# A merged value operand, one channel summed on GpSimd, and row sums inverted by chunk in an attention kernel

## The chip, the cores and the metric

One core of a Trainium2 chip. The metric is the device time of one execution in microseconds (us), lower is better. The engines are TensorE (PE in the rows; PEld is its weight load), VectorE (DVE), ScalarE (ACT), GpSimd (POOL) and SyncE (SP), which here issues the DMAs of the attention.

## The reference, cut to what matters

One step of a hybrid encoder: a combined input projection, a short gated convolution, a forgetting attention, and an output projection with a norm. The change touches the attention over the 2,048 prompt rows, for 8 heads of 64 channels:

```
logits = einsum('bqhd,bkhd->bhqk', q, k) * scale
logits = logits + cq[..., None] - ck[:, :, None, :]
logits = where(k_pos <= q_pos, logits, -inf)
att = einsum('bhqk,bkhd->bqhd', softmax(logits), v)
y_b = att * silu(z_b)
```

## The kernel before, in words

The program has two stages. The first makes the projections and writes q, k and v, each split into a high and a low part, to DRAM. The second runs the prompt attention, then the attention of 32 sample rows over a cache (`sample_attention`), the merge and the output norm. All matrix products take split operands: high x high, high x low and low x high.

`prompt_attention` runs over heads h = 0 to 7. A head has NS = 40 steps (q, kb): four chunks q of QW = 512 queries, and for each the key blocks kb = 0 to 4q + 3 of 128 keys. So the chunks take 4, 8, 12 and 16 steps, and `ends` = (3, 11, 23, 39) are their last steps. The last four key blocks of a chunk lie on the diagonal and are narrower (512, 384, 256 and 128 columns). In a step

- TensorE (`tensor`) makes the logits of step st + 3 (`scores`, two passes), units of the row maxima of the *next* head (`unit`, 40 a head, spread over steps 0 to 29, in two banks `m_bank` by turns), and then the values of step st (`values`, three passes into `o_bank[q % 2]`);
- ScalarE (`probs`) takes the exponential of a step twice: rounded into `p_hi`, and full into the logits' own bank;
- VectorE makes the low part (`low`, into `p_lo`), reduces the units, and at the end of a chunk copies the output out of PSUM (`take`).

p_hi, p_lo and the logits' banks are rings of RING = 4. The value operand `v_hi` holds 64 channels of high values and columns of ones, so that row 64 of the output is the sum of the probabilities; `v_lo` holds 64 channels of low values and zeros.

The row sums must be inverted and spread over 64 partitions. That goes through DRAM on SyncE's queue: `sum_store` (a row of 512 sums to DRAM), `sums_load` (back as 128 x 16), `invert` on VectorE (step INVERT = 9 of the next head), `rcp_store`, `rcp_load` (broadcast). Then GpSimd and ScalarE finish the head in steps 20 to 37 of the next one: `scale`, `gate`, `upper` (high part) and `lower` (low part); `y_store` writes both parts.

SyncE works through its list strictly in the order written in `sync`: a DMA behind a wait, or behind a DMA whose issue is held, waits too. `load_main(h + 1)` loads keys, queries and values of the next head, `load_max(h + 2)` what the row maxima of the head after need. Lines of the program before, with the profile's numbers: L1531 and L1533 are the loads of `load_main`, L1525 those of `load_max`, L1502 the sum store, L1507 and L1515 the loads of sums and reciprocals, L1605 to L1607 the value passes, L1588 and L1589 the logits, L1621 a unit, L1667 and L1668 the exponentials, L1698 the low part, L1706 the reduction of a unit, L1651 `upper`, L1767 to L1776 GpSimd's finishing, L1901 the cached keys for the sample part.

Of the kernel before, what the change touches and what calls it, by code (L numbers as in the profile page):

```python
# [23 lines left out]
H = 8  # L24
# [177 lines left out]
def front(nc, held, s, g_out, lead, x_prompt, x_sample, ln_in, w_tiles, w_f, b_f, conv_w, cache_logf, state_conv, ident, causal,  # L202
          k_prompt, v_prompt, logf_prompt, conv_prompt, k_sample, v_sample, logf_sample, conv_sample):
    with ExitStack() as ctx:
# [148 lines left out]
        def _(sp):  # L353
# [139 lines left out]
            for i in range(NSETS + 2):  # L493
# [90 lines left out]
                if i == 2 * PER + 19:  # L584
                    load_lead_v(0, s["vh"])
# [747 lines left out]
        def _(pool):  # L1333
# [16 lines left out]
            pool.memset(v0[0][:, :, HD:P].bitcast(F32), 1.0).then_inc(lead_ones, 1)  # L1350
            for idx in (0, 2, 5):
                pool.wait_ge(w_lo[idx], NSETS - 1)
            pool.memset(v0[1][:, :, HD:P].bitcast(F32), 0.0).then_inc(lead_ones, 1)
# [58 lines left out]
def prompt_attention(nc, held, s, g_out, lead, causal):  # L1412
    st_ = Stage()
    with ExitStack() as ctx:
# [21 lines left out]
        v_hi, v_lo = (main[:, :, 2 + x].rearrange("p a (b c) -> p a b c", c=P) for x in range(2))  # L1436
# [16 lines left out]
        o_read = sem("o_read")  # L1453
        sum_out, sums_in, rcp_done, rcp_out, rcp_in = (
            sem("sum_out"), sem("sums_in"), sem("rcp_done"), sem("rcp_out"), sem("rcp_in"))
# [15 lines left out]
        INVERT = 9  # L1471
        FINISH = {20 + 4 * q + x + x // 2: (q, x) for x in range(3) for q in range(NQ)}
        FINISH_LOW = {st + 5: q for st, (q, x) in FINISH.items() if x == 0}
        TURN = 32

# [24 lines left out]
        def sum_store(sp, h, q):  # L1500
            sp.wait_ge(o_read, NQ * h + q + 3)
            sp.dma_start(s["sums"][h:h + 1, q * QW:(q + 1) * QW], y[HD:HD + 1, h % 2, q * QW:(q + 1) * QW])\  # L1502
              .then_inc(sum_out, 16)

        def sums_load(sp, h):
            sp.wait_ge(sum_out, 64 * h + 64)
            sp.dma_start(sums[:, :], s["sums"][h:h + 1, :].rearrange("a (p b) -> (a p) b", p=P)).then_inc(sums_in, 16)  # L1507

        def rcp_store(sp, h):
            sp.wait_ge(rcp_done, h + 1)  # L1510
            sp.dma_start(s["rcps"][h:h + 1, :].rearrange("a (p b) -> (a p) b", p=P), rcp[:, :]).then_inc(rcp_out, 16)

        def rcp_load(sp, h):
            sp.wait_ge(rcp_out, 16 * h + 16)
            sp.dma_start(rcp_all[:, :], s["rcps"][h:h + 1, :].broadcast_to([HD, SEQ])).then_inc(rcp_in, 16)  # L1515
# [4 lines left out]
        def sync(sp, sam):  # L1520
# [6 lines left out]
            def load_main(h):  # L1527
# [4 lines left out]
                for to, of in ((v_hi, s["vh"]), (v_lo, s["vl"])):  # L1532
                    sp.dma_start(to[:, b, :, 0:HD].bitcast(F32), of[0:SEQ, rows].rearrange("(b p) c -> p b c", p=P))\  # L1533
                      .then_inc(main_in[b], 16)

            for h in range(H):
                if h == 0:
                    sp.dma_start(mask[:, :], causal).then_inc(const_in, 16)
                if h:
                    sum_store(sp, h - 1, 3)  # L1540
                    sums_load(sp, h - 1)
                    rcp_store(sp, h - 1)
                    rcp_load(sp, h - 1)
                sp.dma_start(zb[:, h % 2], s["zb"][h * HD:(h + 1) * HD, 0:SEQ]).then_inc(zb_in[h % 2], 16)
                if h + 1 < H:
                    if h:
                        sp.wait_ge(pv_done, NS * h + RING)
                    load_main(h + 1)
# [6 lines left out]
                if h == H - 1:  # L1555
                    sam.key_loads(sp)
                sum_store(sp, h, 0)
                sum_store(sp, h, 1)
                if h:
                    y_store(sp, h - 1, 0)  # L1560
                sum_store(sp, h, 2)
                if h:
                    y_store(sp, h - 1, 1)
                if h + 1 < H:
                    max_rows(sp, h + 1)
                if h:
                    y_store(sp, h - 1, 2)
                    y_store(sp, h - 1, 3)

        def tensor(pe):  # L1570
            def scores(h, b, st):
# [4 lines left out]
                if st == 0:  # L1576
# [5 lines left out]
                    if h:  # L1582
                        pe.wait_ge(main_in[b], used(h, 2, 96))
                        pe.wait_ge(m_in[h % 3], used(h, 3, 32))
# [9 lines left out]
            def values(h, b, st):  # L1594
# [3 lines left out]
                if h == 0 and st == 0:  # L1598
                    pe.wait_ge(lead.v_in, 32)
                if kb == 0:  # L1600
# [27 lines left out]
            def head(h, b, more=True, ahead=True):  # L1628
                for st in range(NS):
# [9 lines left out]
                    values(h, b, st)  # L1639

# [3 lines left out]
            for h in range(H):  # L1644
                head(h, h % 2, h < H - 1, h < H - 1)

# [8 lines left out]
        def scalar(act):  # L1655
# [5 lines left out]
            def probs(h, st):  # L1661
# [4 lines left out]
                act.wait_ge(pv_done, NS * h + st + 1)  # L1666
                act.activation(p_hi[:, r, cols], s_bank[r][:, cols], ACT.Exp, scale=SCALE)  # L1667
                act.activation(s_bank[r][:, cols], s_bank[r][:, cols], ACT.Exp, scale=SCALE).then_inc(p_done, 1)  # L1668

# [6 lines left out]
            for h in range(H):  # L1676
                for st in range(NS):
# [3 lines left out]
                    if st in FINISH and FINISH[st][1] == 2 and h:  # L1681
                        upper(act, h - 1, 1 - h % 2, FINISH[st][0])

        def invert(dve, h):
            dve.wait_ge(sums_in, 16 * h + 16)
            if h:
                dve.wait_ge(rcp_out, 16 * h)
            dve.reciprocal(rcp[:, :], sums[:, :]).then_inc(rcp_done, 1)
# [3 lines left out]
        def vector(dve, sam):  # L1692
# [32 lines left out]
            def take(h, b, q):  # L1725
                dve.wait_ge(pv_done, NS * h + ends[q] + 1 + RING)
                if h > 1:
                    dve.wait_ge(yl_done, NQ * (h - 1))
                dve.tensor_copy(y[:, b, q * QW:(q + 1) * QW], o_bank[q % 2][0:HD + 1, :]).then_inc(o_read, 1)

            def head(h, b, more=True):
                for st in range(NS):
# [9 lines left out]
                    if st - 2 in ends[:-1]:  # L1742
                        take(h, b, ends.index(st - 2))
                    if b and st == 1:
                        take(h - 1, 1 - b, NQ - 1)
                    if st == INVERT and h:
                        invert(dve, h - 1)
                if b:
                    take(h, b, NQ - 1)

            dve.memset(wide_mask[:, 0:QW - P], 0.0).then_inc(mask_made, 1)
# [4 lines left out]
            for h in range(H):  # L1756
# [3 lines left out]
                head(h, h % 2, h < H - 1)  # L1760

        def scale(pool, h, b, q):
            if q == 0:
                pool.wait_ge(rcp_in, 16 * h + 16)
                pool.wait_ge(zb_in[b], 16 * (h // 2 + 1))
# [15 lines left out]
        def gpsimd(pool, sam):  # L1781
# [3 lines left out]
            pool.memset(v_hi[:, 1, :, HD:P].bitcast(F32), 1.0).then_inc(ones_set, 1)  # L1785
            pool.memset(v_lo[:, 1, :, HD:P].bitcast(F32), 0.0).then_inc(ones_set, 1)
# [3 lines left out]
            for h in range(1, H):  # L1790
                for st in range(NS):
                    if st in FINISH_LOW:
                        lower(pool, h - 1, 1 - h % 2, FINISH_LOW[st])
                    if st in FINISH and FINISH[st][1] < 2:
                        (scale, gate)[FINISH[st][1]](pool, h - 1, 1 - h % 2, FINISH[st][0])
# [5 lines left out]
def sample_attention(nc, held, s, att, cache_k, cache_v, blocks):  # L1801
    me = Stage()
    with ExitStack() as ctx:
# [206 lines left out]
        def vector(dve, mrg):  # L2010
# [15 lines left out]
            for c in range(NP):  # L2026
# [5 lines left out]
                if c == 0:  # L2032
                    att.invert(dve, H - 1)
# [517 lines left out]
def tail_loads(sp, s, att, sam, mrg, out):  # L2551
# [3 lines left out]
    att.sums_load(sp, h)  # L2555
    sam.load_v(sp, 1)
    att.rcp_store(sp, h)
    sam.load_v(sp, 2)
    att.rcp_load(sp, h)
# [97 lines left out]
```

## Time and profile before

| | |
|---|---|
| median of 3 runs | 1916.48 us (1916.2 to 1919.73) |
| profiled execution | 1916.35 us |
| its span on the core | 1914.3 us |
| TensorE busy | 1864.5 us, 97% |
| VectorE busy | 1294.4 us, 68% |
| ScalarE busy | 854.5 us, 45% |
| GpSimd busy | 186.0 us, 10% |
| prompt attention | about 1074 to 1484 us of the span |

Shares are averages over stages with different limits, so the rows of the prediction are taken from the attention alone. TensorE's matmuls are pipelined: a matmul's own time is longer than the distance of two starts, and the distance is what one costs.

### The profile page before, as it was taken

To read this page: it belongs to the slowest core of one execution; us is meant where nothing else is said; L and a number is where in the kernel's file an instruction comes from. 1 tells how busy PE (TensorE), PEld (TensorE's weight loads), DVE (VectorE), ACT (ScalarE), POOL (GpSimd) and SP (SyncE) were. 2 spreads that over 40 slices of the span, in tenths; PEclk is the share of its full clock that TensorE was granted. 3 is DMA by queue.
4 is the path that set the end of the run, shared out by engine and by line. 5 is a ranking of instruction groups with operands and counts; after the bars stand their busy time and mean duration, and the time that the engine had idled before them with its cause. 6 is when DMAs were issued, how large, how long until landed. Compare 5 with 4: busy or idle time off the path is not lost. (4 is left out here: it accounts for less than half of the span.)

```text
span 1914.3 us, 28697 instructions
## 1 busy us (share of the span) xinstructions
PE 1864.5 (97%) x10592; PEld 1725.4 (90%) x10592; DVE 1294.4 (68%) x2256; ACT 854.5 (45%) x1592; POOL 186.0 (10%) x153
## 2 busy tenths in 40 slices
PE   5999999999999999999999999999999999999998
PEld 4999999999999999999999787887788799998885
DVE  7888787954445455544556588889996644457887
ACT  4554555634343444424323577777779700111100
POOL 1000000000000000000000203333323400000111
PEclk8999999999999999999999999999999999999999
DMA  5698898878888886979897906666655697765441
GB/s 200 233 316 303 313 315 297 304 244 307 276 312 295 294 283 230 297 231 325 259 305 237 232 11 133 134 133 134 128 106 147 205 377 245 246 181 162 143 146 72
DMA packets 272782, 435.99 MB, mean 228 GB/s; under 512 B 63252, under 2 KB 139188, under 8 KB 268508
## 3 DMA queue, kind: packets, MB, share of 16 engines
q1 hardware_dynamic: 266884, 425.64, 70.8%
q10 hardware_dynamic: 5760, 8.52, 1.2%
q8 instruction: 85, 1.39, 0.3%
q14 instruction: 53, 0.43, 0.1%
HBM read 285.18 MB, written 148.78 MB: 227 GB/s over the span
## 5 line engine op out<-in xcount | busy, mean ns | idle before, releaser
L781 ACT ACTIVATE fr_wq<-fr_raw 128x512 fp32r<-128x512 f32 x288 | 178.9, 629 | 209.8 <-PE fr_d L625 137.6
L1698 DVE TENSOR_TENSOR at_p_lo<-at_s,at_p_hi 128x512 fp32r<-128x512 f32 (+1 forms) x320 | 192.1, 604 | 42.8 <-ACT at_s L1668 41.2
L1667 ACT ACTIVATE at_p_hi<-at_s 128x512 fp32r<-128x512 f32 (+1 forms) x320 | 170.3, 532 | 83.5 <-PE at_s L1589 49.2
L1045 DVE TENSOR_TENSOR fr_wq<-fr_raw,fr_wq 128x512 fp32r<-128x512 f32 x288 | 192.5, 684 | 9.6 <-ACT fr_wq L781 6.3
L623 PE MATMUL fr_b<-fr_xh,fr_wq 128*128 128x348 f32 x576 | 188.1, 327 | 6.9 <-DVE fr_u L1152 3.9
L623 PE MATMUL fr_c<-fr_xh,fr_wq 128*128 128x348 f32 x576 | 187.5, 325 | 3.8 <-DVE fr_wq L1045 2.8
L623 PE MATMUL fr_a<-fr_xh,fr_wq 128*128 128x348 f32 x576 | 187.2, 325 | 2.2 <-ACT fr_p L854 2.2
L624 PE MATMUL fr_a<-fr_xl,fr_wq 128*128 128x348 f32 x576 | 186.7, 324 | 0.0
L624 PE MATMUL fr_c<-fr_xl,fr_wq 128*128 128x348 f32 x576 | 186.1, 323 | 0.0
L625 PE MATMUL fr_a<-fr_xh,fr_wq 128*128 128x348 f32 x576 | 186.1, 323 | 0.0
L625 PE MATMUL fr_b<-fr_xh,fr_wq 128*128 128x348 f32 x576 | 186.0, 323 | 0.0
L625 PE MATMUL fr_c<-fr_xh,fr_wq 128*128 128x348 f32 x576 | 185.8, 323 | 0.0
L624 PE MATMUL fr_b<-fr_xl,fr_wq 128*128 128x348 f32 x576 | 185.7, 322 | 0.0
L1668 ACT ACTIVATE at_s<-at_s 128x512 f32<-128x512 f32 (+1 forms) x320 | 169.4, 529 | 0.0
L1204 DVE TENSOR_TENSOR fr_res<-fr_c,fr_u 128x348 f32<-128x348 f32 x72 | 37.5, 521 | 182.5 <-PE fr_c L625 182.3
L1605 PE MATMUL at_o<-at_p_hi,at_main 128*128 128x512 f32 (+1 forms) x320 | 123.4, 386 | 0.5
L915 ACT ACTIVATE fr_res<-fr_a 128x348 f32<-128x348 f32 x72 | 33.2, 462 | 193.7 <-PE fr_a L625 186.4
L1706 DVE TENSOR_REDUCE at_piece_max<-at_m 128x1 f32<-128x512 f32 x168 | 114.4, 684 | 6.2 <-PE at_m L1621 5.9
L1588 PE MATMUL at_s<-at_main 128*128 128x512 f32 (+1 forms) x320 | 117.5, 367 | 0.2 <-issue 0.2
L1589 PE MATMUL at_s<-at_qm,at_km 68*128 68x512 f32 (+1 forms) x320 | 117.7, 368 | 0.0
L1606 PE MATMUL at_o<-at_p_lo,at_main 128*128 128x512 f32 (+1 forms) x320 | 117.4, 367 | 0.0
L1607 PE MATMUL at_o<-at_p_hi,at_main 128*128 128x512 f32 (+1 forms) x320 | 117.2, 366 | 0.0
(360 smaller groups left out, 4652.8 us busy)
## 6 DMA issues: line engine op xcount, KB each, us to landing
fr_wq<-w_mixed SPq DMA_DIRECT2D x192, 512.0 KB, 5.4
fr_raw<-w_tiles SPq DMA_DIRECT2D x96, 512.0 KB, 5.3
w_mixed<-fr_wq SPq DMA_DIRECT2D x96, 512.0 KB, 4.6
mg_gates<-merge_gates SPq DMA_DIRECT2D x40, 416.0 KB, 4.8
fr_raw<-w_tiles SPq DMA_DIRECT2D x48, 256.0 KB, 5.7
merge_gates<-fr_res SPq DMA_DIRECT2D x32, 348.0 KB, 6.4
mixed<-mg_mixed ACTq DMA_DIRECT2D x40, 208.0 KB, 4.1
ln_h<-h_rows SPq DMA_DIRECT2D x16, 512.0 KB, 3.2
```

The lines of the kernel that those rows point to most:

```text
L623: pe.matmul(to, wh[:, idx, k, :], xh[:, idx, k, :], start=first, stop=False, skip_group_check=skip)
L624: pe.matmul(to, wh[:, idx, k, :], xl[:, idx, k, :], start=False, stop=False, skip_group_check=skip)
L625: last = pe.matmul(to, wl[:, idx, k, :], xh[:, idx, k, :], start=False, stop=end, skip_group_check=skip)
L781: act.activation(wh[:, idx], operand(i, idx), ACT.Copy).then_inc(w_hi[idx], 1)
L1045: dve.tensor_tensor(wl[:, idx], operand(i, idx), wh[:, idx].bitcast(F32), ALU.subtract).then_inc(w_lo[idx], 1)
L1588: pe.matmul(bank[:, cols], ks[:, b, keys], qs[:, b, asked], start=True, stop=False)
L1589: last = pe.matmul(bank[:, cols], km[h % 3][:, keys], qm[h % 3][:, asked], start=False, stop=not diagonal)
L1605: pe.matmul(o, v_hi[:, b, kb, :], p_hi[:, r, cols], start=(kb == 0), stop=False)
L1606: pe.matmul(o, v_hi[:, b, kb, :], p_lo[:, r, cols], start=False, stop=False)
L1667: act.activation(p_hi[:, r, cols], s_bank[r][:, cols], ACT.Exp, scale=SCALE)
L1668: act.activation(s_bank[r][:, cols], s_bank[r][:, cols], ACT.Exp, scale=SCALE).then_inc(p_done, 1)
L1698: dve.tensor_tensor(p_lo[:, r, cols], s_bank[r][:, cols], p_hi[:, r, cols].bitcast(F32), ALU.subtract)\
```

## The change

Part one joins the operands. `v_both` holds 64 channels of high values, one column of ones, and channels 1 to 63 of the low values. One pass with p_hi and one with p_lo give high values, row sums and 63 low channels. `v_first` holds the low channel 0 and zeros, and is multiplied by p_hi in a third pass as before, except in the "pooled" steps: those below the diagonal with odd kb (kb = 1, 3 for q = 1, up to 1, 3, ..., 11 for q = 3). There GpSimd multiplies p_hi by the channel (`first_channel`) and adds it up in `acc`; one matmul a chunk q = 1, 2, 3 (`close`) sums `acc` over the partitions into the output bank.

Part two: the low rows now lie on partitions 64 to 127 of the output. ScalarE copies them to `part` (`copy_part`), and VectorE's `take` adds them to the high rows. `part` is one buffer; row 64 of it is what `sum_store` sends.

Part three: sums are loaded, inverted, stored and spread by chunk, with tables of steps for each job, and SyncE's list has a new order.

```diff
+                for to, of in ((v_both[:, b, :, 0:HD], s["vh"][0:SEQ, rows]),
+                               (v_both[:, b, :, HD + 1:P], s["vl"][0:SEQ, h * HD + 1:(h + 1) * HD]),
+                               (v_first[:, b, :, 0:1], s["vl"][0:SEQ, h * HD:h * HD + 1])):
...
             for h in range(H):
...
-                if h:
-                    sum_store(sp, h - 1, 3)
-                    sums_load(sp, h - 1)
-                    rcp_store(sp, h - 1)
-                    rcp_load(sp, h - 1)
+                if h > 1:
+                    sp.wait_ge(y_gated, NQ * (h - 1))
                 sp.dma_start(zb[:, h % 2], s["zb"][h * HD:(h + 1) * HD, 0:SEQ]).then_inc(zb_in[h % 2], 16)
                 if h + 1 < H:
                     if h:
-                        sp.wait_ge(pv_done, NS * h + RING)
+                        sp.wait_ge(closed, 3 * h)
                     load_main(h + 1)
                 if h + 2 < H:
...
                     load_max(h + 2)
                 if h == 1:
                     sam.early_loads(sp)
                 if h == H - 1:
                     sam.key_loads(sp)
+                if h:
+                    sum_store(sp, h - 1, 3)
+                    y_store(sp, h - 1, 1)
+                    y_store(sp, h - 1, 2)
+                    sums_load(sp, h - 1, 3)
                 sum_store(sp, h, 0)
+                sums_load(sp, h, 0)
+                if h:
+                    rcp_store(sp, h - 1, 3)
+                    rcp_load(sp, h - 1, 3)
+                rcp_store(sp, h, 0)
                 sum_store(sp, h, 1)
...
-                pe.matmul(o, v_hi[:, b, kb, :], p_hi[:, r, cols], start=(kb == 0), stop=False)
-                pe.matmul(o, v_hi[:, b, kb, :], p_lo[:, r, cols], start=False, stop=False)
-                pe.matmul(o, v_lo[:, b, kb, :], p_hi[:, r, cols], start=False, stop=(kb == 4 * q + 3))\
-                  .then_inc(pv_done, 1)
+                pe.matmul(o, v_both[:, b, kb, :], p_hi[:, r, cols], start=(kb == 0), stop=False)
+                last = pe.matmul(o, v_both[:, b, kb, :], p_lo[:, r, cols], start=False, stop=False)
+                if not pooled(st):
+                    last = pe.matmul(o, v_first[:, b, kb, :], p_hi[:, r, cols], start=False, stop=(q == 0 and kb == 3))
+                last.then_inc(pv_done, 1)
+
+            def close(h, q):
...
+                pe.wait_ge(acc_done, added_through(h, q))
+                pe.matmul(o_bank[q % 2][:, :], first_row[:, :], acc[:, :], start=False, stop=True).then_inc(closed, 1)
...
                     values(h, b, st)
+                    if h and st == 0:
+                        close(h - 1, NQ - 1)
+                    if st - 1 in ends[1:-1]:
+                        close(h, ends.index(st - 1))
...
+                if before[0] >= 0 and pooled(before[1]):
+                    act.wait_ge(acc_scaled, pooled_through(*before))
...
+            def copy_part(h, q):
+                n = NQ * h + q
...
+                act.wait_ge(o_read, n + 2)
+                act.wait_ge(sum_out, 16 * n)
+                act.activation(part[HD:2 * HD, :], o_bank[q % 2][HD:2 * HD, :], ACT.Copy).then_inc(part_done, 1)
...
             def take(h, b, q):
-                dve.wait_ge(pv_done, NS * h + ends[q] + 1 + RING)
+                dve.wait_ge(part_done, NQ * h + q + 1)
...
-                dve.tensor_copy(y[:, b, q * QW:(q + 1) * QW], o_bank[q % 2][0:HD + 1, :]).then_inc(o_read, 1)
+                o = o_bank[q % 2]
+                dve.scalar_tensor_tensor(out=y[0:HD, b, q * QW:(q + 1) * QW], in0=part[HD:2 * HD, :], scalar=lanes[HD:2 * HD, :],
+                                         in1=o[0:HD, :], op0=ALU.mult, op1=ALU.add).then_inc(o_read, 1)
```

The tables, as (head back, chunk) by step: `copy_part` stands at steps 8, 16, 28 and, for chunk 3, step 4 of the next head; `take` at 7, 15, 27 and 3; `invert` at 15, 23, 35 and 12 of the next head; scale, gate, upper and lower of chunk 0 at 24, 25, 28 and 29, the others in steps 0 to 23 of the next head.

In SyncE's list, this is the turn of one head in the middle of the attention, before. `at_main` is what `load_main` fills, `at_km` and `at_qm` belong to `load_max`:

```order
L1502 DMA sums<-at_y 1x512
L1507 DMA at_sums<-sums 128x16
L1511 DMA rcps<-at_rcp 128x16
L1515 DMA at_rcp_all<-rcps 64x2048
L1544 DMA at_zb<-silu_zb 64x2048
L1531 DMA at_main<-k_hi 64x2048
```

And now, from the first load of the head to the first sum stores:

```order
L1574 DMA at_zb<-silu_zb 64x2048
L1562 DMA at_main<-k_hi 64x2048
L1562 DMA at_main<-q_lo 64x2048
L1562 DMA at_main<-k_lo 64x2048
L1562 DMA at_main<-q_hi 64x2048
L1566 DMA at_main<-v_hi 128x16x64
L1566 DMA at_main<-v_lo 128x16x63
L1566 DMA at_main<-v_lo 128x16x1
L1556 DMA at_km_51<-k_hi 64x2048
L1556 DMA at_qm_53<-q_hi 64x2048
L1556 DMA at_km_51<-forget_rows 2x2048
L1528 DMA sums<-at_part 1x512
```

The store of the previous head's last sums, first of the head before, now stands behind its loads, and there is one load more (`v_lo 128x16x1`).

On ScalarE, before, around steps 7, 8 and 9 of a head there are only exponentials (a 512 pair, the 512 pair of step 8, the 384 pair of step 9):

```order
L1668 ACTIVATE at_s<-at_s 128x512
L1667 ACTIVATE at_p_hi<-at_s 128x512
L1668 ACTIVATE at_s<-at_s 128x512
L1667 ACTIVATE at_p_hi<-at_s 128x384
L1668 ACTIVATE at_s<-at_s 128x384
```

And now at the same place:

```order
L1727 ACTIVATE at_s<-at_s 128x512
L1726 ACTIVATE at_p_hi<-at_s 128x512
L1727 ACTIVATE at_s<-at_s 128x512
L1737 ACTIVATE at_part<-at_o 64x512
L1726 ACTIVATE at_p_hi<-at_s 128x384
L1727 ACTIVATE at_s<-at_s 128x384
```

The copy of chunk 0 has come between the exponentials of steps 8 and 9, with the waits of `copy_part`.

## Rows read from the trace of the kernel before

**Rows 1.** Head 3 in stretches: busy PE, PEld, DVE, ACT, POOL; granted clock, DMA.
```profile
1235.80:1248.00 12.20, 12.15 (x64) 9.87 (x63) 11.48 (x32) 7.98 (x19) 0.00 (x0) 1.00 0.01 2
1248.00:1261.60 13.60, 13.60 (x67) 11.01 (x67) 13.34 (x30) 10.68 (x21) 3.83 (x3) 1.00 0.76 161
1261.60:1276.80 15.20, 15.20 (x71) 12.15 (x71) 14.59 (x30) 12.36 (x25) 8.66 (x7) 1.00 1.10 210
1276.80:1287.70 10.90, 10.81 (x61) 8.50 (x59) 6.90 (x16) 8.71 (x22) 2.71 (x3) 1.00 0.33 91
```

**Rows 2.** Timeline of TensorE in head 2: start, duration (us).
```profile
1217.59 0.40 PE L1605 MATMUL at_o<-at_p_hi,at_main 128*128 128x512 f32 x1
...
1218.06 0.39 PE L1607 MATMUL at_o<-at_p_hi,at_main 128*128 128x512 f32 x1
```

**Rows 3.** Timeline of SyncE's queue in head 3: start and time of issue.
```profile
1251.73 0.59 SPq L1531 DMA_DIRECT2D at_main<-k_hi  x1
...
1254.93 12.66 SPq L1533 DMA_DIRECT2D at_main<-v_lo  x1
...
1271.12 0.54 SPq L1502 DMA_DIRECT2D sums<-at_y  x2
```

**Rows 4.** DMA issues of 1199 to 1235 us: size, time to landing (us).
```profile
at_rcp_all<-rcps SPq DMA_DIRECT2D x1, 512.0 KB, 4.7
...
at_main<-k_hi SPq DMA_DIRECT2D x1, 512.0 KB, 8.6
...
at_main<-v_hi SPq DMA_DIRECT2D x1, 512.0 KB, 16.0
at_main<-v_lo SPq DMA_DIRECT2D x1, 512.0 KB, 18.6
```

**Rows 5.** Groups of ScalarE and VectorE by shape: busy us, mean ns.
```profile
L1706 DVE TENSOR_REDUCE at_piece_max<-at_m 128x1 f32<-128x512 f32 x168 | 114.4, 684 | 6.2 <-PE at_m L1621 5.9
...
L1698 DVE TENSOR_TENSOR at_p_lo<-at_s,at_p_hi 128x384 fp32r<-128x384 f32 x32 | 17.7, 553 | 1.4 <-ACT at_s L1668 0.3
...
L1651 ACT ACTIVATE at_y_hi<-at_y 64x512 fp32r<-64x512 f32 x32 | 19.6, 618 | 0.0
...
L1668 ACT ACTIVATE at_s<-at_s 128x384 f32<-128x384 f32 x32 | 15.5, 486 | 0.0
```

**Rows 6.** GpSimd's `lower`: shortest, median and longest duration (ns).
```profile
L1776 POOL TENSOR_TENSOR at_y_lo<-at_y,at_y_hi x32: 1278/1284/2335, 1159.6 to 1521.6; 64x512 fp32r<-64x512 f32 x32
```

**Rows 7.** Waits of SyncE in the attention: total us, times, longest.
```profile
SPq L1507 <- DMA sums<-at_y: 6.3, 7, 0.9
```

**Rows 8.** Timeline of TensorE in head 3: first value pass, step 9's first unit.
```profile
1235.85 0.45 PE L1605 MATMUL at_o<-at_p_hi,at_main 128*128 128x512 f32 x1
...
1247.82 0.40 PE L1621 MATMUL at_m<-at_km,at_qm 66*128 66x512 f32 x1
```

**Rows 9.** Timeline of TensorE where the attention stage begins, with its idle before.
```profile
1073.95 0.22 PE L1641 MATMUL at_m<-at_eye_b,at_mask_b 128*128 128x128 bf16 x1 [3.42 <-PEq L65]
```

**Rows 10.** Stretches of 2 us in head 0, columns as in rows 1.
```profile
1078.00:1080.00 2.00, 2.00 (x5) 1.70 (x6) 0.65 (x4) 0.36 (x2) 1.37 (x2) 0.50 1.15 326
1080.00:1082.00 2.00, 2.00 (x7) 1.81 (x6) 0.64 (x3) 1.09 (x2) 1.85 (x2) 0.52 1.09 225
1082.00:1084.00 2.00, 2.00 (x13) 1.74 (x12) 1.35 (x5) 1.39 (x3) 0.42 (x1) 1.00 1.00 205
```

**Rows 11.** Timeline of SyncE's queue in head 1, from the early loads on.
```profile
1166.88 1.28 SPq L1889 DMA_DIRECT2D sa_q_hi<-q_hi  x2
...
1174.76 0.35 SPq L1502 DMA_DIRECT2D sums<-at_y  x1
```

**Rows 12.** Timeline of SyncE's queue in head 7.
```profile
1454.90 4.71 SPq L1901 DMA_DIRECT2D sa_k_rows<-cache_k  x4
...
1464.12 0.56 SPq L1502 DMA_DIRECT2D sums<-at_y  x2
```

**Rows 13.** Line L1901, the cached keys: issue to landing.
```profile
DMA to landing us min/median/max: 9.3/12.5/17.4
```

More of the change, by code:

```diff
@@ L1435, in prompt_attention @@
         ks, qs = main[:, :, 0], main[:, :, 1]
-        v_hi, v_lo = (main[:, :, 2 + x].rearrange("p a (b c) -> p a b c", c=P) for x in range(2))
+        v_both, v_first = (main[:, :, 2 + x].rearrange("p a (b c) -> p a b c", c=P) for x in range(2))
+        first_row = sb("first_row", [P, P], 29184, F32R)
+        acc = sb("acc", [P, QW], 29312, F32R)
+        lanes = sb("lanes", [P, 1], 29824)
+        part = sb("part", [P, QW], 34880)
+        term = sb("term", [P, QW], 29832)
         s_bank = [pb(f"s{i}") for i in range(RING)]
@@ L1469, in step_units, with pooled, pooled_through, added_through @@
             return range(min(NU, st * 4 // 3), min(NU, (st + 1) * 4 // 3))
-        INVERT = 9
-        FINISH = {20 + 4 * q + x + x // 2: (q, x) for x in range(3) for q in range(NQ)}
-        FINISH_LOW = {st + 5: q for st, (q, x) in FINISH.items() if x == 0}
-        TURN = 32
+        INVERT = {15: (0, 0), 23: (0, 1), 35: (0, 2), 12: (1, 3)}
+        SCALE_AT = {24: (0, 0), 0: (1, 1), 2: (1, 2), 18: (1, 3)}
+        GATE_AT = {25: (0, 0), 1: (1, 1), 3: (1, 2), 19: (1, 3)}
+        UPPER_AT = {28: (0, 0), 4: (1, 1), 6: (1, 2), 22: (1, 3)}
+        LOWER_AT = {29: (0, 0), 5: (1, 1), 7: (1, 2), 23: (1, 3)}
+        PART_AT = {(e + 5) % NS: (0 if e + 5 < NS else 1, q) for q, e in enumerate(ends)}
+        TAKE_AT = {(e + 4) % NS: (0 if e + 4 < NS else 1, q) for q, e in enumerate(ends)}
+        TURN = 32
+        def pooled(st):
+            q, kb = steps[st]
+            return kb < 4 * q and kb % 2 == 1
+        def pooled_through(h, st):
+            return sum(map(pooled, range(NS))) * h + sum(map(pooled, range(st + 1)))
+        def added_through(h, q):
+            return pooled_through(h, ends[q]) - 3 * h - q
+        def at_step(plan, h, st):
+            back, q = plan.get(st, (0, None))
+            h -= back
+            return (h, q) if q is not None and h >= 0 else None
         def used(h, slots, per):
@@ L1741, in head @@
                             whole_max(h + 1)
[L1742 to L1749, printed above, removed]
+                    job = at_step(TAKE_AT, h, st)
+                    if job:
+                        take(job[0], job[0] % 2, job[1])
+                    if at_step(INVERT, h, st):
+                        invert(dve, *at_step(INVERT, h, st))
+            dve.memset(lanes[:, :], 1.0).then_inc(lanes_set, 1)
+            dve.wait_ge(lanes_set, 1)
+            dve.memset(lanes[HD:HD + 1, :], 0.0).then_inc(lanes_set, 1)
+            dve.wait_ge(lanes_set, 2)
             dve.memset(wide_mask[:, 0:QW - P], 0.0).then_inc(mask_made, 1)
@@ L1784, in gpsimd @@
             pool.wait_ge(ones_set, 2)
[L1785 to L1786 removed]
+            pool.memset(v_both[:, 1, :, HD:HD + 1].bitcast(F32), 1.0).then_inc(ones_set, 1)
+            pool.memset(v_first[:, 1, :, 1:P].bitcast(F32), 0.0).then_inc(ones_set, 1)
+            pool.memset(first_row[:, 1:P].bitcast(F32), 0.0).then_inc(first_row_set, 1)
+            pool.memset(first_row[:, 0:1].bitcast(F32), 1.0).then_inc(first_row_set, 1)
             for q in g_out:
@@ L2032, in vector @@
                 if c == 0:
[L2033 removed]
+                    att.invert(dve, H - 1, NQ - 1)
                 if c:
```

139 lines of the change are left out of this document (92 added, 47 removed).

## Prediction

> **What bounds the kernel now.** I read the busy time of one head by stretches first. Attention runs eight heads of 40 steps; head 3 (counted from 0) takes the 51.9 us from 1235.8, cut at its steps 9, 19 and 30 [rows 1]. TensorE is busy 51.76 of 51.90 us at full granted clock, so it sets the pace. VectorE is right behind in steps 9 to 29: 13.34 of 13.60 and 14.59 of 15.20 us, which leaves 0.87 us. ScalarE has 2.2 us left in the last ten steps; GpSimd is nearly idle. Then the timeline of TensorE: two passes of 512 columns lie 1217.59 to 1218.06 apart, so one costs 0.235 us [rows 2].
>
> Then SyncE's queue, which looks harmless now [rows 3]. The loads for head 4 begin at 1251.73, the issue of v_lo holds the queue for 12.66 us, and the store of row sums behind them is issued at 1271.12, after 19.4 us. The landing times say why: k_hi, q_lo, k_lo and q_hi move first and v_hi lands 16.0 us after its own issue [rows 4]; the queue takes v_lo's 2,048 small pieces only as those before them drain. Nobody waits for that store today: `take` has copied the sums to `y`, and the inversion comes a head later.
>
> **The change part by part.**
>
> *Passes.* A step below the diagonal with odd kb loses its third value pass: 2 + 4 + 6 = 12 of 40. Three closings per head come back. Net 9 x 0.235 = 2.1 us a head, 16.9 us in all, if nothing else binds. In steps 9 to 29 seven passes go and two closings come (1.2 us), where VectorE has 0.87 us and gets three more small inversions; I keep 0.6 there, 0.24 in steps 0 to 8, 0.55 of 0.7 at the end beside ScalarE. That is 1.4 a head: **11 us gained** (ends 5 and 16.9).
>
> *ScalarE and VectorE.* `copy_part` moves 64x512 out of PSUM, near the 64x512 ACTIVATE of 0.62 us [rows 5]; four a head, in ScalarE's idle time except where it waits (below). `take` stays one 512-wide VectorE instruction. Nothing for either.
>
> *GpSimd.* A pooled step costs a multiply and an add of 128x512. Nearest row: 64x512 two-input, median 1.28 us [rows 6]. Steps 24 to 35 ask for 6 multiplies, 5 adds and 3 finishing operations: 14 x 1.3 = 18.2 us, against about 13.2 us of TensorE. ScalarE comes back to a slot of the ring of four after four steps (4.8 us); less the multiply itself, GpSimd may be about 3.5 us late. At 1.3 us a multiply it would be 5.0 late: 1.5 us a head, 12 in all. At half that price a multiply (one input) costs 0.65 and nothing stalls. I take nothing, with 0 and 12 as ends.
> The Trainium skill (GPSIMD Engine Reference, section Elementwise — side-by-side cycle accounting) gives a two-input operation about 2.6 cycles per element, which would be 1.1 us (the row shows 1.28), and a one-input loop at best 769 ns for 512 elements. By that estimate the stretch asks 15.0 us, nothing stalls and the sum stays as below; by 1.3 us for both it is 12 us more.
>
> *The order of SyncE's queue; this decides.* Now the loads of head h+1 stand first in head h, and the store of the last row sums of head h-1 behind them. `part` is one buffer: `copy_part` of (h, 0), which stands on ScalarE after step 8, waits until all 4h earlier stores have landed. That store cannot be issued before the loads, and the loads wait for the last closing of head h-1, which TensorE does in step 0 of head h. From the first value pass of head h, in us:
> - three passes, the closing and its end: SyncE is released at 1.2;
> - the loads: 19.4 as now [rows 3], less 3.9, since rcp_all and zb are no longer in front (k_hi lands 8.6 after its issue, a 512 KB transfer with an empty queue 4.7 [rows 4]), plus the new load of 2,048 pieces of 4 bytes. No row has that. v_lo's 2,048 pieces of 256 bytes land 2.6 after v_hi's and were issued 0.63 later: 3.2. Ends: 0 and 6; I take 3.0, near the row with as many pieces. So 18.5: the store is issued at 19.7;
> - it lands 1.1 later (0.2 of issue, 0.9 of SyncE's wait [rows 7]): 20.8;
> - ScalarE's copy 0.6: 21.4. Behind it stand the two exponentials of step 9 (384 wide, 0.49 each, overlapping: 0.9): 22.3. VectorE, held in `take`, then makes p_lo (0.55): 22.85, and reads unit 10 (0.6): 23.4 [rows 5].
>
> TensorE cannot pass: the values of step 9 need that p, and its first unit of step 9 needs unit 10's bank. Now it comes to that unit at 1247.82, 12.0 after 1235.85 [rows 8]; two passes fewer make it 11.5. So TensorE stands **11.9 us in each head**. After an idle of 3.42 us at the change of stages [rows 9] the granted clock was half (1.2 GHz): 5 and 7 matmuls in two windows of 2 us at 0.50 and 0.52, then 13 in one at 1.00 [rows 10]. That is some 2 us lost; after a stall VectorE is late as well and hides a little of it. I add 1.7 us a stall (ends 0 and 2): 13.6.
>
> *Which heads.* Heads 2 to 6: 5 x 13.6 = 68.0. Head 1 has the early loads of the sample part ahead of the store too, 1166.88 to 1174.76 = 7.9 [rows 11]: 21.5. Head 7 loads cached keys instead, 9.2 from the first key load to the store [rows 12], so the store goes out 10.4 sooner; with no units TensorE is at step 9 about 2 sooner: 3.4. There the inversion of (6, 3) on VectorE in step 12 waits for sums that lie behind 4 MB of keys, the last of which lands 17.4 after its issue [rows 13]: about 3 more. 6.5 together (0 to 12).
>
> *Edges.* One more small load ahead of head 0 and a copy ahead of the last `take`: about 1 us each (0 to 3 together). Head 0 has no earlier store to wait for.
>
> **Sum.** 68.0 + 21.5 + 6.5 + 2 - 11 = +87. The profiled execution took 1916.35 us (span 1914.3 and 2.05 around it), as good as the median of 1916.48. So **2003 us**. Its ends: with 0 for the 4-byte load, no loss of clock, the full gain and nothing in head 7 or at the edges, the idle is 8.9 and the sum 6 x 8.9 + 7.9 - 16.9 = +44 (1961). With 6 for it, half the relief, 2 of clock, 5 gained and 12 in head 7, it is 6 x 18.8 + 7.9 + 12 + 3 - 5 = +131 (2047).
>
> **Rivals.**
> - *It does what it says.* The queue takes the loads at once when nothing is in front, the store is out in time, and the gain less the edges is left: 1916 - 9 = 1907. It decides where the loads are issued within 18.5 - 11.9 = 6.6 us of the closing. For it: seven loads at 0.6 us would be 4.2. Against: four transfers of 512 KB, landing some 2.5 us apart, still stand before v_hi. 9%.
> - *The queue blocks, but half as long*, because it is empty at the start: issued after 12 instead of 18.5, TensorE stands 5.4 us: 6 x 5.4 + 7.9 + 3 + 2 - 11 = +34, 1950. For: the block is data, and 1 MB less is ahead. Against: 1 MB was worth 3.9 us and is already off. 9%.
> - *GpSimd becomes the bound.* The longest two-input operation took 2.34 us [rows 6]. If all did, steps 24 to 35 would ask 14 x 2.3 = 32 against 13, 15 us a head past what the ring forgives: 120 on top, 2123. Against: the median is 1.28 while VectorE was nine tenths busy. 5%. The Trainium skill (GPSIMD Engine Reference, Key points) says that GpSimd shares its SBUF interfaces with VectorE and contends with VectorE instructions that have two SBUF inputs; those of the steps have one input in PSUM, and by that rule they do not slow it.
>
> **How the numbers follow.** The forecast with its ends has 75%, the three rivals 9, 9 and 5, and 2% is left for what I do not see. Likeliest 2003, alone 1961 to 2047; the range goes down to 1940 to take in the half block and up to 2045. About 0.2% (4 us) is what a measurement of this kernel can tell from no change. Slower by more: 0.89; within: 0.02; faster: 0.09.
>
> **What would show it.** Right: in heads 1 to 6 an idle of 9 to 17 us on TensorE before the first unit of step 9, ScalarE's `at_part` copy of (h, 0) waiting for the DMA of `sums`, SyncE's issue of the v loads still held 8 us or more, heads of about 64 us, and a granted clock near 0.5 for some us after each. Also 96 value passes fewer, 24 closings, the multiply on GpSimd under 1.3 us. Wrong: the store of (h-1, 3) issued within 7 us of the closing, or POOL named as what ScalarE waits for.

## The result and the profile after

| | before | after |
|---|---|---|
| median of 4 runs each, same chip | 1916.34 us (1915.47 to 1919.73) | 2081.43 us (2079.32 to 2082.36) |
| ratio, 95% interval | | 1.086 (1.0845 to 1.0875) |
| span of the profiled execution | 1914.3 us | 2080.5 us |
| mean granted clock of TensorE | 0.989 | 0.953 |
| GpSimd busy | 186.0 us | 426.9 us |

The change costs 165 us. The forecast was 2003, from 1940 to 2045: the sign and the place were right, the size about half.

The first value pass of each head, in the timeline of TensorE, gives the length of the heads. Head 7 and the last column are divided at the first value pass of its last step. The lower lines are kernels of the experiments.

| us | head 0 | 1 | 2 | 3 | 4 | 5 | 6 | 7 | rest |
|---|---|---|---|---|---|---|---|---|---|
| before | 53.3 | 52.4 | 51.9 | 52.0 | 51.9 | 51.9 | 51.8 | 40.5 | 430.3 |
| after | 63.2 | 79.7 | 74.8 | 75.5 | 75.2 | 74.3 | 67.8 | 57.4 | 433.5 |
| e5, only SyncE's list mended | 55.7 | 57.4 | 56.8 | 56.8 | 56.8 | 57.1 | 58.3 | 49.3 | 431.9 |
| e6, copy of chunk 3 earlier | 55.9 | 57.1 | 56.5 | 56.5 | 56.4 | 56.7 | 56.5 | 49.5 | 435.2 |
| e7, and no channel on GpSimd | 55.2 | 53.9 | 55.3 | 54.8 | 54.7 | 54.4 | 54.3 | 41.5 | 436.4 |
| e11, list mended again | 54.5 | 53.4 | 55.3 | 53.3 | 53.4 | 53.4 | 53.2 | 42.6 | 432.1 |
| e12, before with the new order | 54.3 | 68.3 | 65.3 | 64.9 | 64.9 | 66.7 | 59.2 | 49.2 | 433.9 |

All but some 4 us of the loss lies in the attention. Its third value pass of 512 columns runs 128 times in place of 224, and 24 closings have come, as foretold. Head 3 in stretches, cut by what happens there (columns as in [rows 1]):

```profile
1297.00:1308.80 11.80, 10.69 (x55) 8.59 (x56) 9.67 (x26) 7.81 (x17) 10.45 (x9) 1.00 0.85 182
1308.80:1325.40 16.60, 1.43 (x7) 0.85 (x6) 2.13 (x4) 2.88 (x9) 0.37 (x1) 0.64 0.90 161
1325.40:1334.40 9.00, 9.00 (x27) 7.56 (x28) 5.83 (x14) 3.78 (x8) 0.23 (x1) 0.53 0.02 3
```

For nearly 15 us hardly any engine works, only the DMA engines do (0.90 of their time), and then TensorE runs some 9 us at a granted clock near half. SyncE's queue in the same head (start, time of issue), to hold against [rows 3]:

```profile
1298.16 0.45 SPq L1562 DMA_DIRECT2D at_main<-k_hi  x1
...
1301.21 11.68 SPq L1566 DMA_DIRECT2D at_main<-v_lo  x2
1312.93 2.25 SPq L1556 DMA_DIRECT2D at_km<-k_hi  x1
...
1316.35 0.25 SPq L1528 DMA_DIRECT2D sums<-at_part  x1
...
1322.41 0.35 SPq L1533 DMA_DIRECT2D at_sums<-sums  x1
```

The sum store of head 2's last chunk is issued 18.2 us after the first load. Four stores of finished parts follow it without a wait (1316.65 to 1319.05, not shown); the load of those sums, which waits for it to land, goes out at 1322.41: the store of 2 KB took 6.1 us. What it holds up, in the timelines of ScalarE, VectorE and TensorE (in brackets the idle before):

```profile
1322.49 0.59 ACT L1737 ACTIVATE at_part<-at_o 64x512 f32<-64x512 f32 x1 [16.72 <-DMA sums<-at_part]
...
1323.12 0.74 DVE L1803 SCALAR_TENSOR_TENSOR at_y<-at_part,at_lanes,at_o 64x512 f32<-64x512 f32 x1 [14.79 <-ACT at_part L1737]
1324.02 0.56 DVE L1771 TENSOR_TENSOR at_p_lo<-at_s,at_p_hi 128x384 fp32r<-128x384 f32 x1 [0.15 <-ACT at_s L1727]
1324.49 0.68 DVE L1779 TENSOR_REDUCE at_piece_max<-at_m 128x1 f32<-128x512 f32 x1
...
1325.23 0.79 PE L1672 MATMUL at_m<-at_km,at_qm 66*128 66x512 f32 x1 [15.17 <-DVE at_piece_max L1779]
```

This is the chain of the forecast, link by link: store, copy, addition, low part, unit, TensorE. The long idles of the heads that differ from head 3 (heads 0, 1, 6 and 7, the last with two):

```profile
1108.82 0.80 PE L1672 MATMUL at_m<-at_km,at_qm 66*128 66x512 f32 x1 [4.34 <-DVE at_piece_max L1779]
...
1174.88 0.79 PE L1672 MATMUL at_m<-at_km,at_qm 66*128 66x512 f32 x1 [17.81 <-DVE at_piece_max L1779]
...
1544.29 0.80 PE L1672 MATMUL at_m<-at_km,at_qm 66*128 66x512 f32 x1 [9.27 <-DVE at_piece_max L1779]
...
1607.17 0.69 PE L1649 MATMUL at_o<-at_p_hi,at_main 128*128 128x384 f32 x1 [5.54 <-DVE at_p_lo L1771]
...
1626.88 0.33 PE L1649 MATMUL at_o<-at_p_hi,at_main 128*128 128x128 f32 x1 [3.98 <-DVE at_p_lo L1771]
```

Head 0, which was to have no stall, has one at step 17: its own first store stands behind the loads, and the copy of chunk 1 waits for that. GpSimd's groups, to hold against [rows 6]:

```profile
L1886 POOL TENSOR_SCALAR at_term<-at_p_hi,at_main 128x512 f32<-128x512 f32 x72 | 112.6, 1564 | 11.5 <-ACT at_s L1727 6.1 <-POOL at_acc L1888 5.5
L1888 POOL TENSOR_TENSOR at_acc<-at_acc,at_term 128x512 fp32r<-128x512 f32 x72 | 92.7, 1287 | 6.0
L1881 POOL TENSOR_SCALAR at_acc<-at_p_hi,at_main 128x512 fp32r<-128x512 f32 x24 | 37.6, 1567 | 192.7 <-PE at_o L1659 173.0 <-ACT at_s L1727 19.7
```

The multiply costs 1.56 us, more than the two-input addition of 1.29. ScalarE's waits for GpSimd in the attention (total us, times, longest):

```profile
ACT at_y_hi L1707 <- POOL at_y L1849: 31.1, 14, 5.2
...
ACT at_p_hi L1726 <- POOL at_term L1886: 14.8, 10, 1.9
```

The first is `upper`, which waits for a part that GpSimd has gated, the second an exponential that waits for its slot of the ring.

### The profile page after: what moved, and what is told of

It is laid out like the page before. It is cut to its first block and busy times, and to the rows that moved or that the text cites. A ratio compares the mean times of both kernels' runs of the same rounds, so it can differ in the third digit from the quotient of the medians.

```text
span 2080.5 us, 29040 instructions
## 1 busy us (share of the span) xinstructions
PE 1896.1 (91%) x10520; PEld 1737.7 (84%) x10520; DVE 1313.8 (63%) x2282; ACT 868.2 (42%) x1624; POOL 426.9 (21%) x323
## 5 line engine op out<-in xcount | busy, mean ns | idle before, releaser
L1771 DVE TENSOR_TENSOR at_p_lo<-at_s,at_p_hi 128x512 fp32r<-128x512 f32 (+1 forms) x320 | 193.0, 605 | 68.3 <-ACT at_s L1727 66.2
L1672 PE MATMUL at_m<-at_km,at_qm 66*128 66x512 f32 (+2 forms) x280 | 112.7, 427 | 102.6 <-DVE at_piece_max L1779 102.6
L626 PE MATMUL fr_b<-fr_xh,fr_wq 128*128 128x348 f32 x576 | 186.0, 323 | 0.0
L1672 PEld LDWEIGHTS at_m<-at_km,at_qm 66*128 66x128 f32 x280 | 57.6, 208 | 128.9 <-DVE at_piece_max L1779 118.7
L1649 PE MATMUL at_o<-at_p_hi,at_main 128*128 128x512 f32 (+1 forms) x320 | 130.5, 408 | 29.0 <-DVE at_p_lo L1771 21.8
L1338 POOL TENSOR_TENSOR fr_small<-fr_small 128x1 f32<-128x1 f32 (+1 forms) x18 | 12.4, 688 | 622.3 <-DVE fr_small L1021 622.3
L1632 PE MATMUL at_s<-at_main 128*128 128x512 f32 (+1 forms) x320 | 124.1, 388 | 0.0
L1633 PE MATMUL at_s<-at_qm,at_km 68*128 68x512 f32 (+1 forms) x320 | 123.5, 386 | 0.0
```

Source lines behind the costliest of these rows:

```text
L626: last = pe.matmul(to, wl[:, idx, k, :], xh[:, idx, k, :], start=False, stop=end, skip_group_check=skip)
L1632: pe.matmul(bank[:, cols], ks[:, b, keys], qs[:, b, asked], start=True, stop=False)
L1649: pe.matmul(o, v_both[:, b, kb, :], p_hi[:, r, cols], start=(kb == 0), stop=False)
L1672: pe.matmul(bank[:, 0:width], qm[h % 3][0:HD + 2, i * P:(i + 1) * P], km[h % 3][0:HD + 2, c * QW:end], start=True, stop=True).then_inc(uni ...
L1771: dve.tensor_tensor(p_lo[:, r, cols], s_bank[r][:, cols], p_hi[:, r, cols].bitcast(F32), ALU.subtract)\
```

## The experiments

Theory A: the order of SyncE's list makes the loss, through the late store. B: the added work on GpSimd and VectorE makes it. C: the single buffer `part` makes it. D: the store lands late whatever stands ahead of it. Times are medians of 4 runs; the kernel before, run beside each of them on the same chip, stood at 1915.5 to 1916.7.

**e12, the order alone in the kernel before.**

```diff
-                if h:
-                    sum_store(sp, h - 1, 3)
-                    sums_load(sp, h - 1)
-                    rcp_store(sp, h - 1)
-                    rcp_load(sp, h - 1)
-                sp.dma_start(zb[:, h % 2], s["zb"][h * HD:(h + 1) * HD, 0:SEQ]).then_inc(zb_in[h % 2], 16)
...
                     load_main(h + 1)
...
                     load_max(h + 2)
...
                     sam.key_loads(sp)
+                if h:
+                    sum_store(sp, h - 1, 3)
+                    sums_load(sp, h - 1)
+                    rcp_store(sp, h - 1)
+                    rcp_load(sp, h - 1)
+                sp.dma_start(zb[:, h % 2], s["zb"][h * HD:(h + 1) * HD, 0:SEQ]).then_inc(zb_in[h % 2], 16)
```

> The kernel before, and of the whole change only the order in SyncE's list: the loads for the next heads stand ahead of the store, load and spreading of the last head's sums. Theory A (the order by itself makes the greater part of the loss): the sums come back some 25 us into each head, VectorE inverts them at step 9 (about 12 us in) and waits, TensorE stands 10 to 14 us in heads 1 to 6 and runs some us at half clock after it: 1990 to 2040 us. Rival (the order costs nothing without the copy that waits for the store): 1916, no change.

Measured: 2003.89 us, ratio 1.0453 (1.0432 to 1.0473). Nothing but the list is changed, and 88 us are lost. (`zb` comes last here; in the change it comes first.) SyncE's queue, VectorE and TensorE in head 3:

```profile
1281.98 0.25 SPq L1502 DMA_DIRECT2D sums<-at_y  x1
1287.91 0.35 SPq L1507 DMA_DIRECT2D at_sums<-sums  x1
...
1289.55 0.25 DVE L1688 RECIPROCAL at_rcp<-at_sums 128x16 f32<-128x16 f32 x1 [11.38 <-DMA at_sums<-sums]
...
1290.60 0.80 PE L1621 MATMUL at_m<-at_km,at_qm 66*128 66x512 f32 x1 [11.03 <-DVE at_piece_max L1706]
```

Without `part` and its copy it is the inversion of step 9 that waits. TensorE stands 14.0 us in head 1, 11.0 to 11.6 in heads 2 to 5 and 5.2 in head 6, which has no `load_max`. Theory A holds: which instruction waits differs between the kernels, the late sums do not.

**e2, four buffers, the list as changed.**

```diff
-        part = sb("part", [P, QW], 34880)
+        parts = [sb(f"part{i}", [P, QW], 34880 + i * QW) for i in range(NQ)]
...
-                act.wait_ge(sum_out, 16 * n)
+                act.wait_ge(sum_out, 16 * max(0, n - 3))
```

> The changed kernel with four buffers for the low rows, one for each chunk, so that ScalarE's copy waits only for the store four copies back. SyncE's list is as in the changed kernel. Theory A (the order of the queue): the copy no longer waits, but the sums of the last chunk still come back some 27 us after the head begins, and VectorE, which inverts them at step 12 (about 15 us in), takes the wait over: some 11 us of idle a head in place of 15, about 2050 us (2030 to 2070). Rival C (the one buffer is the cause): the stalls are gone and the time is about 1950 us.

Measured: 2024.59 us, ratio 1.0575 (1.0556 to 1.0595): 57 us better than the change and far from rival C, but 25 better than theory A's 2050 and below its range, since TensorE's idle is some 8 us and not 11. What wait is left went where A put it. VectorE and TensorE in head 3:

```profile
1305.12 0.18 DVE L1761 RECIPROCAL at_rcp<-at_sums 128x4 f32<-128x4 f32 x1 [8.11 <-DMA at_sums<-sums]
...
1306.32 0.80 PE L1672 MATMUL at_m<-at_km,at_qm 66*128 66x512 f32 x1 [7.65 <-DVE at_piece_max L1782]
```

**e4, only the loads for the maxima behind the store.**

```diff
-                if h + 2 < H:
...
-                    load_max(h + 2)
...
                     sum_store(sp, h - 1, 3)
+                    if h + 2 < H:
+                        load_max(h + 2)
```

> The changed kernel, only the loads for the row maxima (two of 512 KB and a small one) stand behind the store of the last sums instead of ahead of it (in head 0 behind the first store). Theory A, with the store landing late because 1 MB stands ahead of it in the same queue: in heads 1 to 5 the store is issued 3.4 us sooner and lands in 1 to 2 us instead of 6.1, so the idle at step 9 falls from 15 to about 7 us and the time to about 2040 us (2025 to 2050). Rival D (the store lands 6 us after its issue whatever stands just ahead): only the 3.4 us come back, 15 to 20 us in all, about 2062 us.

Measured: 2050.01 us, ratio 1.0705 (1.0688 to 1.0723), at the upper edge of A's range; D's 2062 lies outside the interval. SyncE, ScalarE and TensorE in head 3:

```profile
1296.55 1.86 SPq L1528 DMA_DIRECT2D sums<-at_part  x1
...
1300.16 0.59 ACT L1738 ACTIVATE at_part<-at_o 64x512 f32<-64x512 f32 x1 [9.88 <-DMA sums<-at_part]
...
1302.89 0.79 PE L1673 MATMUL at_m<-at_km,at_qm 66*128 66x512 f32 x1 [8.33 <-DVE at_piece_max L1780]
```

From the start of the store's issue to the copy it is now 3.6 us (1.9 of them held issue), not 6.1, and TensorE's idle is 8.3, not 15.2. So what stands ahead in the queue delays not only the issue but also the landing. Head 6, which has no such loads in the changed kernel either, stood 9.27 there. The stores of finished parts behind it do not make the delay: e12 has none there, and its store took 5.9.
The Trainium skill (DMA: Bandwidth & Descriptors, section Queues, rings and completion order) says that SyncE owns one row of rings and that each DMA engine takes that row's descriptors in order. By that rule the small store is taken up after the loads ahead of it; the 6.1 and 3.6 us agree.

**e1, the loads moved behind the stores.** The order of a head is now: last sums of the head before (store, load), `load_max`, sums of chunks 0 and 1, then the block `zb` and `load_main`, then the `y_store`s, sums of chunk 2, `max_rows`.

> Only SyncE's list is changed: the last sums of the head before are stored and loaded first, then come the two large loads for the row maxima, and the gate values and the keys, queries and values of the next head wait until the sums of chunk 1 have been stored and loaded (step 16). Every engine's work is that of the changed kernel. Theory A (the order of the queue makes the loss): ScalarE's copy never waits for a store, TensorE's idle of 15 us at step 9 goes and with it some 4 us of half clock behind it, so a head of 75 takes about 56 and the program 1940 to 1970 us. Rival B (the added work on GpSimd and VectorE makes the loss): the idle moves elsewhere and the time stays above 2010 us.

Measured: 2011.74 us, ratio 1.0505 (1.0484 to 1.0526): a miss for A, and by its words B (above 2010). The idle at step 9 is gone, but this list made a wait of its own, which neither had foreseen. SyncE's queue in head 3:

```profile
1326.26 1.22 SPq L1517 DMA_DIRECT2D at_qm<-at_neg_rows  x2
```

And a wait of TensorE in the attention (total us, times, longest):

```profile
PE at_s L1634 <- issue: 39.2, 6, 7.4
```

The rows of the maxima, ready at 1317.5, stood in the list behind the stores of finished parts and the sums and reciprocals of chunks 1 and 2, until 1326.26, and the first logits of the next head need them. **e3** is e1 without GpSimd's channel (`pooled` false, no `close`).

> As the run with the list in new order, and GpSimd's channel is taken out: every step has three value passes again and no closing, so GpSimd only finishes heads. Theory A (TensorE sets the pace once the stalls are gone): nine passes a head of 0.235 us come back, 17 us more than that run. Rival B (GpSimd's multiplies of 1.56 us and additions of 1.29 us hold the others up): the same time as that run or less.

Measured: 2010.25 us (1.0467 to 1.0524), the same as e1. By the expectation that is B, but both stood at step 37 for the same DMA, so it settles little.

**e5, e1's list mended.** The sums of chunk 2 and `max_rows` ahead of the `y_store`s; half of the cached keys earlier (not shown).

```diff
-                if h:
-                    y_store(sp, h - 1, 1)
-                    y_store(sp, h - 1, 2)
-                    y_store(sp, h - 1, 3)
...
                 if h + 1 < H:
                     max_rows(sp, h + 1)
...
+                if h:
+                    y_store(sp, h - 1, 1)
+                    y_store(sp, h - 1, 2)
+                    y_store(sp, h - 1, 3)
```

> Only SyncE's list differs from the changed kernel. As in the run with the list in new order, but the rows of the maxima for the next head are written before the finished parts are stored, since in that run they came 5 to 8 us late at step 37 of every head; in head 7 half of the cached keys is loaded ahead of the first sum store. Theory A (the order of the queue makes the loss): no idle over 3 us is left on TensorE inside the heads, a head takes 54 to 56 us, and the program 1940 to 1960 us. What then remains above the kernel before, 25 to 45 us, is not the queue but the ordinary steps, 3.3 us a head by the earlier run. Rival: with the stalls gone the time falls to the kernel before or below it (1916 or less), as if the new steps cost nothing.

Measured: 1962.13 us, ratio 1.0246 (1.0229 to 1.0263). SyncE's list alone gives back 119 of the 165 us. That is 2 us above A's range; heads take 57 us, and one idle over 3 us is left, 3.95 in head 7. 46 us are left that the forecast had as a gain of 9.

**e6, copy and addition of the last chunk one step earlier.**

```diff
-        PART_AT = {(e + 5) % NS: (0 if e + 5 < NS else 1, q) for q, e in enumerate(ends)}
-        TAKE_AT = {(e + 4) % NS: (0 if e + 4 < NS else 1, q) for q, e in enumerate(ends)}
+        PART_AT = {(e + 5 - q // 3) % NS: (0 if e + 5 < NS else 1, q) for q, e in enumerate(ends)}
+        TAKE_AT = {(e + 4 - q // 3) % NS: (0 if e + 4 < NS else 1, q) for q, e in enumerate(ends)}
```

> As the run with the mended list, and the copy and the addition of the last chunk of the head before stand one step earlier (copy at step 3, addition at step 2). Theory: the wait of 1.1 us that TensorE has for VectorE's addition before step 4, and the jump of 2.1 us there, come from this chain; one step earlier gives back 1.0 to 1.5 us a head, 8 to 12 us in all. Rival (VectorE's load, not the place of the addition, sets these steps): no change.

Measured: 1959.53 us (1.0213 to 1.0244), 2.6 us less, with single runs that overlap: nearer the rival than the 8 to 12. **e7** takes GpSimd's channel out of e6, as e3 did, and **e8** leaves it 7 of 12 steps:

```diff
-            return kb < 4 * q and kb % 2 == 1
+            return kb < 4 * q and kb % 2 == 1 and (q == 1 or kb % 4 == 1)
```

> As the run with the earlier copy, with GpSimd's channel taken out: three value passes in every step, no closing. Rival B (GpSimd's 3.1 us for a multiply and an addition, every second step, hold back steps 24 to 36): the same time or up to 12 us less than with the channel. Theory A (TensorE sets the pace there): nine passes a head come back, 10 to 17 us more.

> As the run with the earlier copy, but only 7 of the 12 steps of a head go to GpSimd (kb = 1 and 3 of chunk 1, 1 and 5 of chunk 2, 1, 5 and 9 of chunk 3); the other five have their third pass on TensorE again. Rival B (GpSimd is the bound of steps 24 to 36 with all twelve): GpSimd has slack, ScalarE no longer waits for a multiply, and the time is 6 to 12 us below the run with all twelve. Theory A (TensorE sets the pace): five passes a head of 0.235 us come back, 9 us more.

Measured: 1939.77 us (1.0109 to 1.0140) and 1938.63 us (1.0103 to 1.0133). With nine more matmuls a head TensorE is 20 us earlier: rival B, and by more than it said. GpSimd in the last chunk of head 3, in e5 (its steps there are those of e6):

```profile
1295.20 1.56 POOL L1890 TENSOR_SCALAR at_term<-at_p_hi,at_main 128x512 f32<-128x512 f32 x1
1296.84 1.28 POOL L1892 TENSOR_TENSOR at_acc<-at_acc,at_term 128x512 fp32r<-128x512 f32 x1
1298.29 1.57 POOL L1890 TENSOR_SCALAR at_term<-at_p_hi,at_main 128x512 f32<-128x512 f32 x1 [0.17 <-POOL at_acc L1892]
1299.94 1.28 POOL L1892 TENSOR_TENSOR at_acc<-at_acc,at_term 128x512 fp32r<-128x512 f32 x1
1301.39 1.57 POOL L1890 TENSOR_SCALAR at_term<-at_p_hi,at_main 128x512 f32<-128x512 f32 x1 [0.17 <-POOL at_acc L1892]
```

One pooled step follows the other after 3.1 us without a pause. Two steps of e7 take 2.8 us there (its steps 25 to 33 of head 3 in 11.3 us), with a pass less about 2.6: by this estimate GpSimd falls behind. And the waits of ScalarE for GpSimd in e6, and the first of them in e8:

```profile
ACT at_y_hi L1711 <- POOL at_y L1853: 31.3, 14, 5.2
...
ACT at_p_hi L1730 <- POOL at_term L1890: 15.4, 10, 1.9
...
ACT at_y_hi L1711 <- POOL at_y L1853: 8.1, 8, 2.0
```

The larger wait is that of `upper`: the finishing work that it needs stands behind multiplies and additions in GpSimd's list, and ScalarE makes no exponentials meanwhile.

In head 7, where TensorE makes no units and comes faster, this costs most: 49.5 us in e6, 41.5 in e7.

**e9, the list mended once more** (on e8: `zb` ahead of the block, `max_rows` ahead of `rcp_load(h, 1)`), **e10** (on e9: copies of chunks 0 to 2 one step earlier) and **e11** (on e10: no channel on GpSimd).

> As the run with 7 of 12 steps on GpSimd, SyncE's list mended once more: the gate values are loaded before the large block, and the rows of the maxima are written ahead of the reciprocals of chunk 1. In the run before, the issue of the block ended 44.8 us into the head and the maxima were 1.5 to 2 us late at step 37. Theory (what is left of the queue): 1.5 to 2 us a head in heads 1 to 6 come back, about 1927 us (1922 to 1932). Rival: the late step 37 has another cause, no change (1936 to 1941).

> As the run with the list mended once more; the copies of chunks 0 to 2 on ScalarE stand one step earlier (steps 7, 15 and 27, as VectorE's additions do), so that VectorE does not wait for a copy that stands behind the next pair of exponentials. Theory (the chain copy, addition, low part costs 0.5 to 0.6 us for each chunk at steps 8, 16 and 28): 1.5 us a head, about 12 us less, near 1915. Rival (the addition's own 0.74 us and the load of VectorE are the cost): no change within 3 us.

> As the run with the copies one step earlier, without GpSimd's channel: three passes in every step, no closing, so that TensorE does the work of the kernel before and what differs from it is the joined operand with its copies and additions, the inversion by chunk and SyncE's list. Theory A (TensorE paces): four passes a head net more than with seven steps on GpSimd, 5 to 8 us more than that run. Rival (VectorE paces): the same. Against the kernel before: what is left above it is the price of copy and addition, 0 to 10 us.

Measured: 1933.32 us (1.0078 to 1.0109), 1934.06 (1.0084 to 1.0114) and 1932.35 (1.0073 to 1.0106). e9 gives 5 us, half of what was expected; e10 nothing, so the place of the copies is not the price; and e11 with three passes everywhere is as fast as e10 with seven steps on GpSimd. The best version stands 16 us above the kernel before with the same matmuls, more than the 0 to 10 expected. What its head 3 has and [rows 8] had not is a wait at step 4, behind copy and addition:

```profile
1247.07 0.47 PE L1653 MATMUL at_o<-at_p_hi,at_main 128*128 128x512 f32 x1 [0.78 <-DVE at_p_lo L1767]
```

Step by step in TensorE's timeline, heads 1 and 3 to 6 of e11 lose 0.95 us behind step 3 and 0.45 behind each of steps 16 and 28, all where the copy and addition of a chunk stand, nothing at the inversions of steps 12, 23 and 35, and gain 0.4 elsewhere.

No version beats the kernel before.

## Why the prediction was right and where it failed

- **The order of SyncE's queue decides: right, and shown** from both sides (e5 gives 119 us back, e12 loses 88 by the order alone). The forecast had 96 for it (68.0, 21.5 and 6.5). By heads, the changed kernel against e5: 81.8 in heads 2 to 6, 22.3 in head 1, 8.1 in head 7 and 7.5 in head 0, which the forecast left out.
- *"The store is issued at 19.7"*: 1316.35 is 19.4 after TensorE's first value pass at 1296.96. The loads, 18.5 by the forecast, took 18.2, but by luck: e12 has the same loads without the one of 4-byte pieces and took 17.1 (1264.86 to 1281.98), not the 15.5 of the forecast, so the new load costs some 1.1 and not 3.0. The two errors cancel.
- *"It lands 1.1 later"*: **failed**, 6.1. The row it came from [rows 7] had no loads between the store and an empty queue. In the changed kernel 1 MB of `load_max` stands just ahead; e4 shows that this is what it waits for. So the first unit of step 9 in head 3 starts 28.3 us into the head, not 23.4. TensorE itself came there at 13.1, not the *"11.5"* of the forecast, which hid 1.6 of it: the idle is 15.2 there, 14.5 to 15.7 in heads 2 to 5, and not 11.9.
- *"I add 1.7 us a stall"* for the clock: mis-sized in four heads. From the first value pass of step 9 to that of step 13 head 3 took 8.6 us and e5 5.1: 3.5 more, and 3.5 to 3.7 in heads 1 to 4, at half clock for 8 to 9 us. In heads 5 and 6 it was 1.5 and 1.7, at half clock for some 4 us, after idles of 15.7 and 9.3. Why head 5 got its clock back sooner than head 3 is not shown.
- *Heads 2 to 6 alike*: head 6 has no `load_max`, and stood 9.27. *"Head 0 has no earlier store to wait for"*: failed; its own first store was late, 4.3 us. Head 7 lost 17 us against the kernel before. The list explains 8.1 of it (6.5 foretold), with the idle of 5.5 at step 9; most of the rest is GpSimd's, with 4.0 at step 23, behind an `upper` that waited 5.2 for it, and e7 gives 8.0 of it back.
- *"GpSimd: I take nothing, with 0 and 12 as ends"*: **failed**. The step is "at half that price a multiply (one input) costs 0.65 and nothing stalls". It costs 1.56, and e6 against e7 puts the whole channel at a loss of 20 us, with nine matmuls a head saved. The forecast priced the ring's slot alone; the larger wait, 31.1 us in the changed kernel, is that of `upper` for finishing work behind the channel. Its own sign of being wrong, POOL named as what ScalarE waits for, was there. The rival that GpSimd becomes the bound was given 5% at 2.3 us an operation; it came true at 1.56 and 1.29, at a smaller price.
  The Trainium skill (GPSIMD Engine Reference, section Elementwise — side-by-side cycle accounting) has 769 ns as the best case of a loop over 512 elements. The trace has 1564, so the measurement decides.
- *"11 us gained"* by fewer passes: **not seen.** e10 makes four matmuls a head fewer than e11 and takes as long. With all twelve steps on GpSimd the time is higher.
- *"ScalarE and VectorE: nothing for either"*: failed by up to 16 us (e11). It is 1.0 to 1.5 us in each of six heads, at the steps where copy and addition stand and not at the inversions; 3.4 in head 2, 2.1 in head 7 and 1.8 behind the attention. How it divides between copy and addition, and what is left in the queue, was not separated and stays open.

The sum: 119 for the queue in place of 96 is 23 too little; 46 for what is left in e5 in place of -9 is 55 (some 20 of it the channel, 3 the earlier copy, 7 the lists and places of e9 and e10, 16 what e11 keeps). Together they are the 78 us between 2003 and 2081.

## What to carry to other kernels

In an in-order DMA queue a store that someone waits for should stand ahead of bulk loads (here 88 to 119 us hung on it), and its price is read from its landing behind the same neighbours, not from a row in which the queue was empty. Look for everyone who waits for the first late item before crediting a new buffer: e2 halved the idle, and the rest only moved. When work is moved to an idle engine, price each operation from below *and* above against the time between two such steps (here 3.1 us against some 2.6), since the engine's mean idleness says nothing about the chunk in which the work is dense, and look for jobs in its list, here the finishing of heads, that now stand behind the new work.

## What was not expected of the hardware

A GpSimd multiply of 128x512 by one value a partition took 1.56 us, the addition of two such tiles 1.29. A store of 2 KB issued behind 1 MB of loads on one queue took 6.1 us to land (5.9 in e12). After 15.2 us of idle TensorE's granted clock was near half, 1.2 GHz, for some 9 us in head 3, more than twice the stretch at the start of the attention [rows 10]; after 15.7 us in head 5 for some 4 us.
The Trainium skill (Perfetto Trace Analysis, section Per-instruction lifecycle) warns that a DMA's row leaves out the movement of the data; the store's row shows 0.25 us, and only the row of the next waiting instruction shows the 6.1.
